# Delta rule inverse on one Trainium2 core: the products of the doubling steps cut into 32-wide column blocks of TensorE

## The reference, cut to what matters

```python
lmat = jnp.where(strict, jnp.einsum('bhnid,bhnjd->bhnij', k_beta, k) * decay, 0.0)
t_inv = lax.linalg.triangular_solve(eye + lmat, jnp.broadcast_to(eye, lmat.shape),
                                    left_side=True, lower=True, unit_diagonal=True)
u = t_inv @ v_beta
w = t_inv @ (k_beta * jnp.exp(g_cum)[..., None])
```

## Time and profile before

| | us |
|---|---|
| three runs | 2734.62, 2735.50, 2735.88 (median 2735.5) |
| the profiled execution, time | 2736.57 |
| the profiled execution, span of the trace | 2734.4 |
| granted TensorE clock, share of full speed | 0.999 |
| TensorE matmul busy | 2715.1 (99%) |
| VectorE busy | 1965.6 (72%) |
| ScalarE busy | 1330.8 (49%) |
| GpSimd busy | 88.9 (3%) |

### The profile page before, as it was taken

The page is one execution under the profiler, slowest core; times in us unless marked ns, Lnnn a source line. Parts: engine busy times, 40 slices in busy tenths (PEclk is TensorE's granted clock), DMA queues, the critical chain, the costliest instruction groups (busy, mean ns, idle before and its releaser), DMA issues.

```text
span 2734.4 us, 45467 instructions
## 1 busy us (share of the span) xinstructions
PE 2715.1 (99%) x16630; PEld 2327.7 (85%) x16630; DVE 1965.6 (72%) x2745; ACT 1330.8 (49%) x1674; POOL 88.9 (3%) x106
## 2 busy tenths in 40 slices
PE   9999999999999999999999999999999999999998
PEld 8888888888888888888888888888888888888887
DVE  7888888868888888644465777757678888885444
ACT  6444555455444444433465555566554444443343
POOL 0110110100000000000000000000000000000000
PEclk9999999999999999999999999999999999999999
DMA  7545445574555555655645543345455555555554
GB/s 249 175 159 168 157 160 162 162 201 154 187 191 191 191 184 184 192 186 191 217 142 171 172 136 124 124 147 185 154 177 187 191 191 193 195 185 185 185 186 153
DMA packets 136190, 481.56 MB, mean 176 GB/s; under 512 B 14880, under 2 KB 19120, under 8 KB 135680
## 3 DMA queue, kind: packets, MB, share of 16 engines
q1 hardware_dynamic: 134160, 472.06, 52.8%
q0 software_dynamic: 1376, 7.46, 0.8%
q10 hardware_dynamic: 528, 0.26, 0.0%
HBM read 477.63 MB, written 2.10 MB: 175 GB/s over the span
## 4 chain that ended last, share of the span: by engine, by line
PE 77%; DVE 9%; issue 5%; ACT 4%; DMA 3%; DVEq 1%; POOL 0%; SPq 0%; ACTq 0%
PE acc L418 26%; PE acc L420 13%; PE acc L441 8%; PE acc L443 8%; PE acc L442 8%; PE acc L389 4%; DVE wts L336 3%; DMA raw<-stream 3%; ACT wts L330 2%; PE acc L391 2%; DVE cy L2224 1%; DVE cin L367 1%; DVE half L355 1%; PE ps L1938 1%; PE ps L1931 1%
## 5 line engine op out<-in xcount | busy, mean ns | idle before, releaser
L418 PE MATMUL acc<-hs,wts 128*128 128x512 f32 x4640 | 1631.5, 395 | 0.0
L336 DVE TENSOR_TENSOR wts<-raw,wts 128x1024 fp32r<-128x1024 f32 x888 | 1058.1, 1222 | 539.6 <-ACT wts L330 538.8
L330 ACT ACTIVATE wts<-raw 128x1024 fp32r<-128x1024 f32 x888 | 912.6, 1054 | 874.4 <-PE acc L420 377.5
L420 PE MATMUL acc<-hs,wts 128*128 128x256 f32 x4640 | 1297.1, 280 | 0.0
L418 PEld LDWEIGHTS acc<-hs,wts 128*128 128x128 f32 x4640 | 871.1, 188 | 192.8 <-issue 0.7
L420 PEld LDWEIGHTS acc<-hs,wts 128*128 128x128 f32 x4640 | 871.7, 188 | 0.8 <-issue 0.7
L441 PE MATMUL acc<-wts,acts 128*128 128x512 f32 x688 | 272.6, 396 | 1.5 <-DVE wts L336 1.4
L443 PE MATMUL acc<-wts,acts 128*128 128x512 f32 x688 | 272.8, 396 | 0.0
L442 PE MATMUL acc<-wts,acts 128*128 128x512 f32 x688 | 270.4, 393 | 0.0
L344 ACT ACTIVATE half<-acc 128x512 f32<-128x512 f32 x161 | 95.3, 592 | 171.2 <-PE acc L420 151.9
L441 PEld LDWEIGHTS acc<-wts,acts 128*128 128x128 f32 x688 | 129.1, 188 | 32.6 <-DVE wts L336 2.4
(11 more groups left out here) (351 smaller groups left out, 2198.1 us busy)
## 6 DMA issues: line engine op xcount, KB each, us to landing
raw<-stream SPq DMA_DIRECT2D x888, 512.0 KB, 4.1
xf<-xT SPq DMA_DIRECT2D x8, 256.0 KB, 5.9
raw<-stream SPq DMA_DIRECT2D x8, 256.0 KB, 6.0
fw<-stream POOLq DMA_DIRECT2D x2, 1024.0 KB, 6.1
fm<-memT POOLq DMA_DIRECT2D x2, 1024.0 KB, 9.0
memr<-memT POOLq DMA_DIRECT2D x1, 2048.0 KB, 8.9
outT<-memr SPq DMA_DIRECT2D x7, 256.0 KB, 2.8
KQ<-masks POOLq DMA_DIRECT2D x1, 448.0 KB, 6.3
```

What stands on the lines that cost most here:

```text
L330: nc.scalar.activation(whi[:, b, :], raw[:, b, :], ACT.Copy).then_inc(hi_ready, 1)
L336: nc.vector.tensor_tensor(wlo[:, b, :], raw[:, b, :], whi[:, b, :].bitcast(F32), ALU.subtract).then_inc(lo_ready, 1)
L418: nc.tensor.matmul(acc[:, 2 * par + n, :], whi[:, b, c:c + P], src[:, kt, :], start=start, stop=False)
L420: mm = nc.tensor.matmul(acc[:, 2 * par + n, 0:T], wlo[:, b, c:c + P], src[:, kt, 0:T], start=False, stop=stop)
```

## The change

All of it is in TensorE's program. y products of levels 0 to 4 and z products of levels 1 to 5 become 16 matmuls each, one for each of the four matrices and each quarter of 32 stationary columns. They write the PSUM partitions of that quarter. The moving side is the 32 columns of the same block (z), or the half of them that y needs (16 columns). z of level 5 takes the neighbouring block of 32 columns. y of level 5 takes only the two right blocks of each matrix (8 matmuls, 32 by 32), y of level 6 only the right half (4 matmuls, 64 by 64), and z of level 6 is 8 matmuls of 64 by 64. What is no longer computed lies outside the blocks that `Tm` and `TT` keep. The steps, waits and semaphore counts stay as they were: still one increment, on the last matmul of each product.

```diff
+        own_blocks = [(a, slice(s, s + 32)) for a in range(4) for s in range(0, P, 32)]
+        def right_blocks(lv):
+            return [(a, slice(s, s + (1 << lv))) for a in range(4) for s in range(1 << lv, P, 2 << lv)]
+        def sibling_block(w, h):
+            s = w.start - h if w.start // h % 2 else w.start + h
+            return slice(s, s + h)
...
-            for a in range(4):
-                mm = nc.tensor.matmul(half_of(ps[:, 0, col(a)], LEVELS - 1, 0), NLT[:, a, :],
-                                      half_of(ident, LEVELS - 1, 0), start=True, stop=True)
+            for a, w in own_blocks:
+                mm = nc.tensor.matmul(half_of(ps[w, 0, col(a)][:, w], LEVELS - 1, 0), NLT[:, a, w],
+                                      half_of(ident[:, w], LEVELS - 1, 0), start=True, stop=True)
...
-                for a in range(4):
-                    mm = nc.tensor.matmul(half_of(ps[:, 0, col(a)], LEVELS - 1 - lv, 0), NLT[:, a, :],
-                                          half_of(Tm[:, a, :], LEVELS - 1 - lv, 0), start=True, stop=True)
+                for a, w in own_blocks if lv < 5 else right_blocks(lv):
+                    if lv < 5:
+                        out, moving = (half_of(b, LEVELS - 1 - lv, 0) for b in (ps[w, 0, col(a)][:, w], Tm[:, a, w]))
+                    else:
+                        n = slice(w.start - (1 << lv), w.start)
+                        out, moving = ps[w, 0, col(a)][:, n], Tm[:, a, n]
+                    mm = nc.tensor.matmul(out, NLT[:, a, w], moving, start=True, stop=True)
...
-                for a in range(4):
-                    mm = nc.tensor.matmul(ps[:, 1, col(a)], Z[:, a, :], Z[:, a, :], start=True, stop=True)
+                for a, w in own_blocks if lv < 6 else ((a, slice(s, s + 64)) for a in range(4) for s in (0, 64)):
+                    n = w if lv < 5 else sibling_block(w, 1 << lv)
+                    mm = nc.tensor.matmul(ps[w, 1, col(a)][:, n], Z[:, a, w], Z[:, a, n], start=True, stop=True)
```

## The result

| | median us | runs | ratio to the kernel before |
|---|---|---|---|
| before, in the same session | 2735.18 | 2734.58 to 2735.88 | |
| changed | 2720.86 | 2720.16 to 2721.19 | 0.9946 [0.9935, 0.9956] |

What follows compares the result with a forecast made beforehand. TensorE was taken to bound the kernel; 11 x 0.31 + 2 x 0.07 = 3.55 us saved a turn, 14.2 for four, took the median from 2735.5 to 2721.3 us, range 2718.5 to 2725.5.

Steps and rivals of the forecast that it cites:

- TensorE bounds the stretch, and what it saves is kept: Delta rule: other engines wait for TensorE, later stages are TensorE-bound too, so the saved 14.2 us stays.
- The price of the new shape, read from the HGRN rows (0.59): z1 to z5 and y0 to y5: 0.59 us each instead of 0.90, from the HGRN part's 16 matmuls of 32 by 32.
- rival 1: Narrow matmuls take turns, each product costing the sum of its loads and matmuls: +29 us, 2764 us; chance 0.02.
- y6 and z6 (0.83): Level 6 products on 64-wide blocks: 0.83 us each instead of 0.90, 0.07 saved each.
- The sum: Savings per turn: 11 x 0.31 + 2 x 0.07 = 3.55 us, 14.2 us for four turns.
- VectorE just in time: Between z1 and z2, VectorE's idle 0.62 us falls to nil; 0.6 us remain before y2, no new TensorE wait.
- GpSimd keeps up, with 0.7 us left: GpSimd's copy ends 2.80 us after z's end, the next z starts 3.48 after it: 0.7 us remain.
- Rival 2: Entering and leaving the narrow shape costs more beside these operands, all products 0.83: 3.6 us saved, 2731.9; chance 0.03.
- Rival 3: VectorE becomes the bound in pieces with taps, late keeps return 3 to 5 us: 2725, up to 2727; chance 0.08.
- Rival 4: y products with 16 moving columns get cheaper, 0.48 us each: 2.2 us more saved, 2719.1; chance 0.05.

Runs made afterwards that it cites:

- halves: Changed kernel with all products up to level 5 as 8 matmuls of 64 stationary columns: 2731.94 us, ratio 0.9982 to the kernel before.
- smallest: Changed kernel with y0 as 4 transposes, y6 and z6 as 8 matmuls of 32 stationary and 64 moving columns: 2720.47 us, ratio 0.9941 to the kernel before.
- all columns moving: Changed kernel with z of levels 1 to 5 moving all 128 columns instead of the own 32: 2734.59 us, ratio 0.9994 to the kernel before.

## Why the prediction was right

- **TensorE bounds the stretch, and what it saves is kept.** Right: the products' savings by starts are 3.61 us a turn and the kernel is 14.3 us faster. No later stage took any back: from z6 of turn 3 to the end were 911.3 us before and are 911.0 now, and from the y0 of turn 0 to that z6 14.4 less.
- **The price of the new shape, read from the HGRN rows (0.59).** Right for z (0.59); y0 to y5 came to 0.57 to 0.59, 0.58 at the median, near the top of the 0.48 to 0.59 that stood for 16 moving columns. Halving the moving side saves 0.01 us: with 16 as with 32 moving columns the pairs of a quarter start 0.032 us apart, and with 64 stationary and 32 moving columns (y in halves) 0.058. So the step goes by the stationary columns, that is by the loads. The 0.028 that rival 1 had put for a 32-wide load, a quarter of 0.11, was a little low. So was the reading of the earlier trace rows as 0.014 a matmul, which counts the four quarters together: within one quarter matmuls start 0.032 apart, more than the 0.025 that was set against it. What the rows rule out is that the quarters pay such a price one after another, and the forecast needs no more than that.
- **y6 and z6 (0.83).** 0.81 for both. The sum was 0.02 high here and 0.01 high for each y, which is the 0.06 us a turn between 3.55 and 3.61. That y6, with half of z6's matmuls but all in one half, costs the same as z6 bears out that the fullest part of the array sets the time. So does y5, 8 matmuls in two quarters, at 0.57 like the 16 of y4.
- **VectorE just in time.** Right in place: at z2 its idle time is gone, and the keep is 0.12 us late. Its wait was forecast at 21 us and is 18.3.
- **GpSimd keeps up, with 0.7 us left.** It does, with 0.44: its copy for z2 of turn 1 ran from 1663.31 for 1.42 us instead of 1.24, and z2 starts at 1665.17. Why it was slower there wasn't looked into.
- **The rivals.** Rival 1's taking turns doesn't happen in this order of matmuls; a part of it does if they are ordered by quarter, 1.03 us and slower than before. Rival 2's 0.83 is near what halves cost (0.79 and 0.82), so it is a price of the width and not of the operands. Rival 3 is not reached, and begins with about 0.4 us more of VectorE's work per keep. Rival 4's 0.48 for y was not reached: 0.58.

## What to carry to other kernels

A product of small diagonal blocks got cheaper on 32-column quarters here because three things held: the moving side shrank with the weights, neighbours in the program went to different quarters, and the work saved outweighed a fixed part of about 0.3 us for leaving and re-entering the wide shape. The first two were taken away one at a time, and each time the product cost more than the wide one. Estimate such a product as that fixed part plus the work of the fullest quarter, and look first whether the same trace holds the shape elsewhere. When an engine's product shrinks, list who had idle time in the same piece: here the next engine in line came within half a microsecond of setting the pace.

## What the runs showed of the hardware that was not expected

- A step of narrow matmuls between wide ones costs about 0.3 us on top of its work (0.28 by the cost of a second set of 16, 0.32 to 0.35 if the work is counted from the starts as below), whether it is 128 or 32 rows deep.
- The order of the same 16 matmuls is worth 0.44 us a product (0.59 against 1.03). Ordered by quarter, only the last three of a quarter's eight pairs run beside the next quarter.
- From one pair of load and matmul to the next of the same quarter, half or whole, the single records show these steps:

| stationary columns | moving columns | step, us | seen in |
|---|---|---|---|
| 32 | 16 or 32 | 0.032 | changed: y0 to y5, z1 to z5 |
| 32 | 64 | 0.056 | smallest: y6 |
| 32 | 128 | 0.109 | all columns moving: z1 to z5 |
| 64 | 32 or 64 | 0.058 | halves: y2; changed: y6, z6 |
| 128 | 64 or 128 | 0.11 | before: y2, z1 |

Eight such steps and the fixed part give the cost of each narrow product above in the changed order; a wide one costs its eight steps, 0.90, and next to nothing more. In these rows the step follows the wider of the two sides.
